# Router row products moved from the routing stage into the two output projections of a flow-matching backbone; filter products in pairs, one root for all filter norms

## The chip, the cores and the metric

One core of one Trainium2 chip runs the whole program. The metric is device time in microseconds (us). The kernel before takes 2402.25 us, the median of 3 runs (2401.37 to 2402.26). Five engines work side by side: TensorE (PE; its weight loads are shown as PEld), VectorE (DVE), ScalarE (ACT), GpSimd (POOL) and SyncE (SP), which here issues most of the DMA transfers. They meet by semaphores.

## The reference, cut to what matters

A trunk of two layers, an mLSTM layer and a Hyena layer, on 512 latent tokens of 1024 features (768 tokens with the context in the first). Behind each layer comes a feed-forward network of 32 experts; a router picks two experts for each token.

```python
def rmsnorm(x, g):
    y = x * rsqrt(mean(x * x, axis=-1) + EPS)
    return y * g

def hyena_filters(L, w1, b1, freq, w2, b2, w3, decay):   # two filters of 1024 channels, 512 taps
    z = sin(freq * (feat @ w1 + b1))                      # 64 wide
    z = sin(freq * (z @ w2 + b2))
    z = z @ w3                                            # 64 -> 2048
    filt = z * exp(-tau[:, None] * decay[None, :])
    return filt * rsqrt(sum(filt * filt, axis=0) + EPS)   # one norm for each channel

def moe_ffn(xt, rg_w, rg_b, re_w, re_b, w13, w2):         # xt: rmsnorm, scale, shift of the rows
    g_prob = softmax(xt @ rg_w + rg_b)                    # 4 groups
    e_logits = (xt @ re_w + re_b)                         # 32 experts, those of the best group count
    e_w, e_idx = top_k(softmax(e_logits_of_group), 2)
    ...                                                   # each token through its two experts:
    y = (silu(x @ w13[e][:, :512]) * (x @ w13[e][:, 512:])) @ w2[e]
```

## The kernel before

Everything is f32, and each product of 128x512 is two MATMUL instructions in the trace. The residual stream `hl` stays in SBUF as [128, 4, 1024]: token tile t (128 tokens) and features. The program is a sequence of stages; each ends with a barrier of all engines, and its order is written out by hand for each engine.

**Layer-0 projection (stage c4, from L1860).** PE multiplies the mixer's output `yT` with `m_out_w` into banks 0 to 3, a bank for each token tile, for feature half n = 0 and then n = 1 (`project`, L1974; `ow` is the weight in four pieces, the first of which lies in `uT`). DVE multiplies each bank with the gate and adds it to `hl` (`add_projection`, L1932 and L1934). In the first half PE also makes the Hyena filters: 16 tiles of 128 taps x 512 channels, each a product over 64 rows (`filter_tile`, L1985); DVE multiplies with the envelope `E`, ACT squares the tile (L1910), and PE sums the squares over the taps with a matrix of ones (`square_column`, L1992). Then DVE takes for each of four channel groups an inverse root of a 128x512 tile (`rsqrt`, L100 to L105) and scales four filter tiles (L1956 to L1960), and SP stores them. SP's small loads stand at the start (L1876 to L1886), and PE's first product waits for them.

**Routing (`route`, L235 on).** SP issues nine loads of 2 MB at the start, the weights of the first three experts (six halves of w13, three of w2), and two small ones, and has nothing else to do. PE turns `hl` tile by tile (L320), DVE copies the turned tiles, PE multiplies them with the scaled router weights (`logits`, L314) and the shift (L326). ACT squares the rows for the norm (L293), DVE takes the root, ACT scales the rows (L296) and stores them for the gathers (L299). From the logits DVE works out the two experts of each token and a table of slots (L373 to L472, from L378 on unchanged by the edit), and POOL gathers the first three blocks of rows (L218).

**Experts (`experts`, L474 on).** There are 36 steps for 32 experts (four experts have two steps) and some more for overflow. Each step turns the gathered rows (L592), multiplies with w13 (L602), turns the hidden block (L610) and multiplies with w2 (L622). SP loads the weights on (`load_w13`, L521; `load_w2`, L526), each load when PE has done with the buffer that it takes. A seventh buffer `w13x` exists only in this stage, and its load waits for nothing.

```python
q, hq = (2 * p + h - NH) // 2, (2 * p + h - NH) % 2
sp.wait_ge(S["up" if hq else "upa"], LAST[q] + 1)
```

**Hyena (`hyena_mix`, L754 on).** Its end is the output projection `project` (L1078) into eight banks, bank g = 2t + n. `residual` (L182, its operations at L189 and L190) adds them to `hl` as they come. After it stands the routing stage of layer 1, and after its experts the final norm.

## Time and profile before

| what | value |
|---|---|
| median of 3 runs | 2402.25 us |
| profiled execution: its own time | 2399.6 us |
| its span | 2397.7 us |
| PE busy | 2071.9 us, 86% |
| DVE busy | 847.0 us, 35% |
| ACT busy | 357.2 us, 15% |
| POOL busy | 237.9 us, 10% |
| DMA, mean over the span | 247 GB/s |

Times in all rows are from the start of the span. PE is the busiest engine over the whole, but the mean hides stages with different limits: the page's slices show 419 GB/s of DMA through most of both expert stages and next to none in the projections. In slices, layer 0's projection lies at 721 to 877 us, its routing at 878 to 938, its experts to about 1434, Hyena to 1820, routing 1 from 1822 to 1881 and its experts to about 2360. A busy share near 1 of PE with a granted clock of 0.50 is half speed: there the same work takes twice as long.

### The profile page before, as it was taken

Reading aid. Unit: us, or ns where it says so; the run is one execution under the profiler, and the core shown is the slowest. Engines: PE = TensorE matmul, PEld = TensorE weight load, DVE = VectorE, ACT = ScalarE, POOL = GpSimd, SP = SyncE. Lnnn points to the kernel's source line nnn. Section 1 sums busy time; section 2 is a strip of 40 time slices with the busy share of each in tenths; the row PEclk is TensorE's granted clock in tenths of the full one; section 3 lists DMA queues with packets and bytes.
Section 4 is the critical chain, followed back from the end, with each engine's and each line's share of the span. In section 5 each row is a group of like instructions: output and inputs, shape, how many; then the busy total and the mean of one; then the engine's idle time right before and its main releaser. Section 6 shows DMA issues by size and latency. Waiting matters only on the chain. (4 is left out here: it accounts for less than half of the span.)

```text
span 2397.7 us, 20742 instructions
## 1 busy us (share of the span) xinstructions
PE 2071.9 (86%) x7536; PEld 923.4 (39%) x7536; DVE 847.0 (35%) x1645; ACT 357.2 (15%) x754; POOL 237.9 (10%) x525
## 2 busy tenths in 40 slices
PE   5999999999949984999797967999997699888882
PEld 2555344444423352443232323444455244323330
DVE  2776401356351574222111214264744322211113
ACT  2111203122201110111111101211101111111111
POOL 0000000000000001222121210000000122112120
PEclk9999999999979976999999998999997799999996
DMA  9897504211003048999999975112015899999994
GB/s 340 297 377 280 199 36 149 97 62 62 1 2 132 18 182 345 397 419 420 419 419 419 414 275 206 53 53 70 18 71 237 338 405 419 419 420 419 419 416 171
DMA packets 182887, 592.82 MB, mean 247 GB/s; under 512 B 23464, under 2 KB 40608, under 8 KB 175401
## 3 DMA queue, kind: packets, MB, share of 16 engines
...
q14 instruction: 51, 0.42, 0.1%
HBM read 571.87 MB, written 42.31 MB: 256 GB/s over the span
## 5 line engine op out<-in xcount | busy, mean ns | idle before, releaser
L602 PE MATMUL bank<-w,xT0e 128*64 128x512 f32 x976 | 222.9, 603 | 24.0 <-DMA w<-in_moe_w 21.0
L602 PE MATMUL bank<-w,xT1e 128*64 128x512 f32 x944 | 215.0, 603 | 21.6 <-DMA w<-in_moe_w 18.7
L1063 PE MATMUL bank<-uhi,wnh 128*128 128x512 f32 x384 | 168.4, 593 | 0.9 <-ACT uhi L842 0.9
L622 PE MATMUL bank<-w,hT0e 128*64 128x512 f32 x592 | 139.8, 614 | 26.6 <-DMA w<-in_moe_w 22.4
L622 PE MATMUL bank<-w,hT1e 128*64 128x512 f32 x576 | 134.9, 610 | 26.6 <-DMA w<-in_moe_w 22.4
L602 PEld LDWEIGHTS bank<-w,xT0e 128*64 128x64 f32 x976 | 78.7, 139 | 162.2 <-issue 136.8
L602 PEld LDWEIGHTS bank<-w,xT1e 128*64 128x64 f32 x944 | 76.4, 139 | 154.2 <-issue 131.4
L1412 PE MATMUL bank<-uT,wo 128*128 128x512 f32 x256 | 132.0, 597 | 0.8 <-ACT uT L1224 0.8
L1749 PE MATMUL bank<-uT,wo 128*128 128x512 f32 x256 | 110.7, 593 | 0.0
L698 DVE COPY hT0e<-bank 128x256 f32<-128x256 f32 x37 | 15.7, 424 | 258.6 <-PE bank L610 258.6
L698 DVE COPY hT1e<-bank 128x256 f32<-128x256 f32 x36 | 15.3, 424 | 258.9 <-PE bank L610 258.9
L1063 PEld LDWEIGHTS bank<-uhi,wnh 128*128 128x128 f32 x384 | 71.8, 190 | 86.9 <-issue 85.8
L1323 DVE SCALAR_TENSOR_TENSOR acc<-adab,cv,acc 128x2048 f32<-128x2048 f32 x35 | 82.2, 2350 | 16.9 <-DMA adab<-in_ada_w 16.1
L218 POOL DMA_INDIRECT xg<-d_v,gix x79 | 83.8, 1061 | 40.6 <-issue 40.6
L1974 PE MATMUL bank<-ow,yT 128*128 128x512 f32 x192 | 84.5, 593 | 0.0
L1800 PE MATMUL bank<-vw,xmh 128*128 128x512 f32 x192 | 83.0, 592 | 0.0
L622 PEld LDWEIGHTS bank<-w,hT0e 128*64 128x64 f32 x592 | 45.0, 140 | 97.7 <-issue 71.7
L622 PEld LDWEIGHTS bank<-w,hT1e 128*64 128x64 f32 x576 | 43.4, 140 | 95.0 <-issue 69.3
L1413 PE MATMUL bank<-uT,wo 128*128 128x256 f32 x256 | 76.1, 379 | 0.0
L676 ACT ACTIVATE sg0e<-bank 128x256 f32<-128x256 f32 x37 | 14.2, 384 | 405.1 <-PE bank L602 405.1
L1561 POOL TENSOR_SCALAR_AFFINE_SELECT PW<-PW 128x128 f32<-128x128 f32 x32 | 10.8, 343 | 630.3 <-ACT PW L1619 629.0
L1413 PEld LDWEIGHTS bank<-uT,wo 128*128 128x128 f32 x256 | 48.6, 190 | 61.2 <-issue 61.2
...
## 6 DMA issues: line engine op xcount, KB each, us to landing
...
```

Of the source, the lines that this page charges most:

```text
L218: g.indirect_dma_start(xg[u][:], None, d_v[l].rearrange("s (h d) -> (s h) d", h=2), bass.IndirectOffsetOnAxis(gix[u][:, 0:1], 0), bounds_c ...
L602: ins = t_.matmul(b[n * C:(n + 1) * C, :].rearrange("c (g f) -> c g f", g=2), xT[:, k, half * C:(half + 1) * C], w13s[i][:, k, n], start=( ...
L622: ins = t_.matmul(b_y[m * C:(m + 1) * C, :], hT[:, k, half * C:(half + 1) * C], w2[:, u, kk, m * 512:(m + 1) * 512], start=(kk == 0), stop ...
L676: a.activation(sg[:], b_gu[u][:, 0:DE // 2], ACT.Silu).then_inc(S["sg"], 1)
L698: v.tensor_copy(hT[:].rearrange("p k n -> p (k n)"), b_h[:, 0:2 * P]).then_inc(S["hT"], 1)
L1063: ins = t_.matmul(bank[i % 2][:], wn[:, q % 2, k, f * P:(f + 1) * P], uh[:, k, :], start=(k == 0), stop=(k == KD - 1))
L1323: ins = v.scalar_tensor_tensor(out=a_, in0=w, scalar=s, in1=a_, op0=ALU.mult, op1=ALU.add)
L1412: t_.matmul(bank[2 * (i % 2)][:], w, uT[:, k, CTX:NTOK], start=(k == 0), stop=(k == KD - 1))
L1413: ins = t_.matmul(bank[2 * (i % 2) + 1][:, 0:CTX], w, uT[:, k, 0:CTX], start=(k == 0), stop=(k == KD - 1))
L1749: ins = t_.matmul(bank[n % 4][:], wo[h % 2][:, k, f * P:(f + 1) * P], uT[:, k, CTX:NTOK], start=(k == 0), stop=(k == KD - 1))
L1800: ins = t_.matmul(b, xmh[:, f, c0:c0 + P], vw[:, f, :], start=(f == 0), stop=(f == FT - 1))
L1974: ins = t_.matmul(bank[t][:], yT[:, i * FT + f, t * P:(t + 1) * P], ow[i][:, f, n * 512:(n + 1) * 512], start=(i == 0 and f == 0), stop=(i ...
```

## The change

The routing stage loses the squares, the row turns, the copies, the router products and the root. They move into the two projections, row tile by row tile: as soon as tile t of `hl` is complete, ACT squares it, PE turns it (`turn_rows`: eight transposes into two banks), ACT and DVE copy one bank each, and PE multiplies with the router weights (`row_logits`: eight products of 36 columns, 16 instructions). The router weights are scaled in place (`router_rows`), `shift_logits` multiplies the shift, and `row_scales` takes the root of the four row norms. For this the second half of layer 0's projection goes through the token tiles one after the other, where it went through the four weight pieces in the outer loop. In the Hyena stage the turns stand between and behind the last banks. The filter products of two channel groups go side by side: their 64 rows lie in the lower and in the upper half of the array, into two banks, so `fw2`, its biases and `fw3` are loaded into both halves, with five more small loads. The squares are added up on DVE in `acc4`, four products with 32 columns of ones sum all four groups into one bank, one `rsqrt` of 128x512 serves all, and four products of one row each spread its result over the partitions. The logits stay in one bank (6 or 0) across the stage's end.

In the diff indentation is shortened.

```diff
+NR = NGRP + NE
+LGB = (6, 0)
+A2c = sbt(top, "A2c", [P, KD]);
+rss = sbt(top, "rss", [P, TL]); rst = [sbt(top, f"rst{i}", [P, TL]) for i in range(2)]
+s_rwa = [sem(f"s_rwa{l}") for l in range(2)]
...
-def residual(dve, own, src, ready, gate, tmp):
+def router_rows(dve, own, l, rwS):
...
+  own(v.scalar_tensor_tensor(out=A2c[:], in0=scale, scalar=1.0, in1=gain, op0=ALU.add, op1=ALU.mult))
+  own(v.tensor_tensor(rwS, rw[:], shift.rearrange("p (k o) -> p k o", o=1).to_broadcast(wide), ALU.mult))
+  v.tensor_tensor(rw[:], rw[:], A2c[:].rearrange("p (k o) -> p k o", o=1).to_broadcast(wide), ALU.mult).then_inc(s_rwa[l], 1)
...
+def row_scales(dve, own):
+  v = nc.vector
+  own(v.tensor_scalar(rss[:], rss[:], 1.0 / D, EPS, ALU.mult, ALU.add))
+  rsqrt(v, own, rst[0][:], rss[:], rst[1][:])
...
+def turn_rows(t, lo, hi):
+  for k in range(KD):
+    ins = nc.tensor.transpose((hi if k >= KH else lo)[:, k % KH * P:(k % KH + 1) * P], hl[:, t, k * P:(k + 1) * P], ident[:])
...
+def row_logits(t, rows, dst):
+  for k in range(KD):
+    ins = nc.tensor.matmul(dst[:, t * NR:(t + 1) * NR], rows[:, k, :], rtab[0][0][:, k, :], start=(k == 0), stop=(k == KD - 1))
...
+def shift_logits(dst, rwS):
+  for k in range(KD):
+    ins = nc.tensor.matmul(dst[:, TL * NR:(TL + 1) * NR], ones[:], rwS[:, k, :], start=(k == 0), stop=(k == KD - 1))
...
-        at_least(act, S["sq"], t)
-        a.activation(junk, hl[:, t, :], ACT.Square, accum_out=ss[:, t:t + 1]).then_inc(S["sq"], 1)
-      act.wait_ge(S["rstd"], 1)
-      for t in range(TL):
-        a.activation(vt[:, t, :], hl[:, t, :], ACT.Copy, scale=ss[:, t:t + 1]).then_inc(S["vsc"], 1)
+        a.activation(vt[:, t, :], hl[:, t, :], ACT.Copy, scale=rss[:, t:t + 1]).then_inc(S["vsc"], 1)
...
-      def logits(k):
-        pe.wait_ge(S["hTv"], k + 1)
-        if k == 0:
-          pe.wait_ge(S["rwa"], 1)
-        for t in range(TL):
-          ins = t_.matmul(bank[2 + t][:, 0:NR], hT[:, k % 2, t * P:(t + 1) * P], rwA[:, k, :], start=(k == 0), stop=(k == KD - 1))
-        return ins.then_inc(S["lps"], 1)
...
-        v.tensor_copy(hT[:, k % 2, :], bank[k % 2][:]).then_inc(S["hTv"], 1)
-        if k == 5:
-          dve.wait_ge(S["sq"], TL)
-          own(v.tensor_scalar(ss[:], ss[:], 1.0 / D, EPS, ALU.mult, ALU.add))
-          rsqrt(v, own, r1[:], ss[:], r2[:])
-          own(v.tensor_copy(r1[:], ss[:]))
-          v.memset(r2[:], 0.0).then_inc(S["rstd"], 1)
...
+      own(v.tensor_tensor(cst[:], lgb[:, TL * NR:(TL + 1) * NR], rb[:], ALU.add))
+      for t in range(TL):
+        lg = lgb[:, t * NR:(t + 1) * NR]
+        v.scalar_tensor_tensor(out=LG[:, t, :], in0=lg[:, 0:NGRP], scalar=rss[:, t:t + 1], in1=cst[:, 0:NGRP], op0=ALU.mult, op1=ALU.add)
+        own(v.scalar_tensor_tensor(out=LE[:, t, :], in0=lg[:, NGRP:NR], scalar=rss[:, t:t + 1], in1=cst[:, NGRP:NR], op0=ALU.mult, op1=ALU.add))
...
+      for t in range(TL):
+        act.wait_ge(S["ro"], t + 1)
+        at_least(act, S["ln"], t)
+        a.activation(rjunk, hl[:, t, :], ACT.Square, accum_out=rss[:, t:t + 1]).then_inc(S["ln"], 1)
+        act.wait_ge(S["tn"], t + 1)
+        at_least(act, S["lg"], t - 1)
+        a.activation(turned[t % 2][:, 0:KH, :].rearrange("p k n -> p (k n)"), bank[2 * t][:], ACT.Copy).then_inc(S["tcA"], 1)
...
-      residual(dve, own, bank, S["o"], g1, A)
+      router_rows(dve, own, 1, rwS)
+      def turned_rows(t):
+        dve.wait_ge(S["tn"], t + 1)
+        at_least(dve, S["lg"], t - 1)
+        v.tensor_copy(turned[t % 2][:, KH:KD, :].rearrange("p k n -> p (k n)"), bank[2 * t + 1][:]).then_inc(S["tcV"], 1)
+      for t in range(TL):
+        for n in range(2):
+          cs = slice(n * 512, (n + 1) * 512)
+          dve.wait_ge(S["o"], 2 * t + n + 1)
+          own(v.tensor_tensor(A[:, n, :], bank[2 * t + n][:], g1[:, cs], ALU.mult))
+          ins = v.tensor_tensor(hl[:, t, cs], hl[:, t, cs], A[:, n, :], ALU.add)
+          if n == 0:
+            own(ins)
+          else:
+            ins.then_inc(S["ro"], 1)
+        if t >= 2:
+          turned_rows(t - 2)
+      turned_rows(TL - 2)
+      turned_rows(TL - 1)
+      dve.wait_ge(S["ln"], TL)
+      row_scales(dve, own)
...
+      def turn(t):
+        pe.wait_ge(S["ro"], t + 1)
+        turn_rows(t, bank[2 * t], bank[2 * t + 1]).then_inc(S["tn"], 1)
+      def logits(t):
+        pe.wait_ge(S["tcA"], t + 1)
+        pe.wait_ge(S["tcV"], t + 1)
+        row_logits(t, turned[t % 2], bank[LGB[1]]).then_inc(S["lg"], 1)
       for g in range(4, 8):
         project(g, range(KD)).then_inc(S["o"], 1)
+        if g == 5:
+          turn(0)
+        if g == 6:
+          pe.wait_ge(s_rwa[1], 1)
+          logits(0)
+          turn(1)
+      logits(1)
+      turn(2)
+      shift_logits(bank[LGB[1]], rwS)
+      logits(2)
+      turn(3)
+      logits(3)
...
-    sp.dma_start(fw2[:], I["h_f_w2"][0]).then_inc(s_fld, 16)
-    for i, k in enumerate(("h_f_b1", "h_f_b2", "h_f_freq")):
-      sp.dma_start(pc[:, i:i + 1], I[k].rearrange("o p -> p o"), allow_slow_non_contiguous=True).then_inc(s_fld, 16)
-    sp.dma_start(fw3[:], I["h_f_w3"][0]).then_inc(s_dec, 16)
+    for h in range(2):
+      sp.dma_start(fw2[:, h, :], I["h_f_w2"][0]).then_inc(s_fld, 16)
+      for i, k in enumerate(("h_f_b1", "h_f_b2", "h_f_freq")):
+        sp.dma_start(pc[h * HFH:(h + 1) * HFH, i:i + 1], I[k].rearrange("o p -> p o"), allow_slow_non_contiguous=True).then_inc(s_fld, 16)
+    for h in range(2):
+      sp.dma_start(fw3[h * HFH:(h + 1) * HFH, :], I["h_f_w3"][0][:, h * D:(h + 1) * D]).then_inc(s_dec, 16)
...
+    for j in range(NP4):
+      n, t = pair(j)
+      if j + 1 < NP4:
+        envelopes(j + 1)
+      act.wait_ge(s_g, 2 * j + 2)
+      at_least(act, s_ac4, n * (TL - 1) + max(t - 1, 0))
+      for h in range(2):
+        a.activation(sqt[:, h, :] if t else acc4[:, n + 2 * h, :], tile(n + 2 * h, t), ACT.Square).then_inc(s_sq4, 1)
+    for t in range(TL):
+      act.wait_ge(s_hl4, t + 1)
+      at_least(act, s_ln, t)
+      a.activation(junk, hl[:, t, :], ACT.Square, accum_out=rss[:, t:t + 1]).then_inc(s_ln, 1)
+      act.wait_ge(s_tn, t + 1)
+      at_least(act, s_lg, t - 1)
+      a.activation(turned[t % 2][:, 0:KH, :].rearrange("p k n -> p (k n)"), bank[4][:], ACT.Copy).then_inc(s_tcA, 1)
...
-    def square_sum(n):
-      dve.wait_ge(s_sm, TL * n + TL)
-      v.tensor_scalar(fsum[:, n, :], bank[6 + n % 2][:], EPS, None, ALU.add).then_inc(s_smv, 1)
...
+    def square_sums(j):
+      n, t = pair(j)
+      dve.wait_ge(s_sq4, 2 * j + 2)
+      if t > 0:
+        for h in range(2):
+          ins = v.tensor_tensor(acc4[:, n + 2 * h, :], acc4[:, n + 2 * h, :], sqt[:, h, :], ALU.add)
+        ins.then_inc(s_ac4, 1)
...
-    for n in range(4):
-      dve.wait_ge(s_smv, n + 1)
-      r = fsum[:, n, :]
-      rsqrt(v, own, kx[:], r, ft[:])
...
+    dve.wait_ge(s_sm, 1)
+    own(v.tensor_scalar(rn, bank[4][:], EPS, None, ALU.add))
+    dve.wait_ge(s_x4, 32)
+    add_projection(0, 0)
+    add_projection(0, 1)
+    rsqrt(v, own, kx, rn, rtmp)
+    v.memset(pc[:, 0:1], 0.0).then_inc(s_rn, 1)
+    add_projection(0, 2)
+    add_projection(0, 3)
+    add_projection(1, 0)
+    normalised(0)
+    normalised(1)
+    normalised(2)
+    add_projection(1, 1)
+    turned_rows(0)
+    normalised(3)
+    for t in range(2, TL):
+      add_projection(1, t)
+      turned_rows(t - 1)
+    turned_rows(TL - 1)
+    dve.wait_ge(s_ln, TL)
+    row_scales(dve, own)
...
-    def filter_tile(i):
-      n, t = i // TL, i % TL
-      if i == 0:
+    def filter_pair(j):
+      n, t = pair(j)
+      if j == 0:
         pe.wait_ge(s_zz, 2)
-        pe.wait_ge(s_dec, 64)
-      at_least(pe, s_g, i - 1)
-      t_.matmul(bank[4 + i % 2][:], z[1][:, t * P:(t + 1) * P], fw3[:, n * 512:(n + 1) * 512], start=True, stop=True).then_inc(s_zps, 1)
-    def square_column(i):
-      n, t = i // TL, i % TL
-      pe.wait_ge(s_sq4, i + 1)
-      if t == 0:
-        at_least(pe, s_smv, n - 1)
-      t_.matmul(bank[6 + n % 2][:], ones[:], sqf[:], start=(t == 0), stop=(t == TL - 1)).then_inc(s_sm, 1)
+        pe.wait_ge(s_dec, 80)
+      at_least(pe, s_g, 2 * j - 2)
+      for h in range(2):
+        rows = slice(h * HFH, (h + 1) * HFH)
+        t_.matmul(bank[4 + 2 * (j % 2) + h][:], z1[rows, t * P:(t + 1) * P], fw3[rows, n * 512:(n + 1) * 512], start=True, stop=True).then_inc(s_zps, 1)
     groups = [(i, t) for i in range(HEADS) for t in range(TL)]
-    pe.wait_ge(s_fld, 16 * 6)
+    pe.wait_ge(s_fld, 160)
     t_.matmul(bank[4][0:HFH, :], fw1[:], ft[0:HEMB, :], start=True, stop=True).then_inc(s_zps, 1)
     for g, (i, t) in enumerate(groups):
       project(0, i, t)
-      if g == 2:
+      if g == 1:
         pe.wait_ge(s_zz, 1)
-        t_.matmul(bank[4][0:HFH, :], fw2[:], z[0][:], start=True, stop=True).then_inc(s_zps, 1)
-      if g >= FIRST:
-        filter_tile(g - FIRST)
-      if g >= FIRST + 1:
-        square_column(g - FIRST - 1)
-    done = len(groups) - FIRST
-    for i in range(done, NT4):
-      filter_tile(i)
-      square_column(i - 1)
-    square_column(NT4 - 1)
-    for i, t in groups:
-      project(1, i, t)
+        t_.matmul(bank[4][:], fw2[:].rearrange("p h n -> p (h n)"), z0[0:HFH, :], start=True, stop=True).then_inc(s_zps, 1)
+      if FIRST <= g < FIRST + NP4:
+        filter_pair(g - FIRST)
+      if g == FIRST + NP4 + 1:
+        pe.wait_ge(s_ac4, 2 * (TL - 1))
+        for n in range(4):
+          ins = t_.matmul(bank[4][32 * n:32 * n + 32, :], ones[:, 0:32], acc4[:, n, :], start=True, stop=True)
+        ins.then_inc(s_sm, 1)
+    for t in range(TL):
+      for i in range(HEADS):
+        project(1, i, t)
+      if t == 0:
+        pe.wait_ge(s_rn, 1)
+        for n in range(4):
+          t_.matmul(bank[4 + n][:], ones[32 * n:32 * n + 1, :], rn[32 * n:32 * n + 1, :], start=True, stop=True).then_inc(s_bc, 1)
+      else:
+        pe.wait_ge(s_hl4, t)
+        pe.wait_ge(s_fin, 2)
+        at_least(pe, s_tcA, t - 1)
+        at_least(pe, s_tcV, t - 1)
+        turn_rows(t - 1, bank[4], bank[5]).then_inc(s_tn, 1)
+      if t >= 2:
+        pe.wait_ge(s_tcA, t - 1)
+        pe.wait_ge(s_tcV, t - 1)
+        if t == 2:
+          pe.wait_ge(s_fin, 3)
+        row_logits(t - 2, turned[t % 2], bank[LGB[0]]).then_inc(s_lg, 1)
+    pe.wait_ge(s_tcA, TL - 1)
+    pe.wait_ge(s_tcV, TL - 1)
+    row_logits(TL - 2, turned[TL % 2], bank[LGB[0]]).then_inc(s_lg, 1)
+    pe.wait_ge(s_hl4, TL)
+    turn_rows(TL - 1, bank[4], bank[5]).then_inc(s_tn, 1)
+    shift_logits(bank[LGB[0]], rwS)
+    pe.wait_ge(s_tcA, TL)
+    pe.wait_ge(s_tcV, TL)
+    row_logits(TL - 1, turned[(TL - 1) % 2], bank[LGB[0]]).then_inc(s_lg, 1)
```

On PE, in the first half of layer 0's projection, the filter products (`fw3`) and square sums (`onesmat`) stood between the projection groups like this (x4 counts four products):

```order
L1974 MATMUL bank1<-ow1,yT 128x512 x4
L1985 MATMUL bank4<-fw3,z1 128x512
L1974 MATMUL bank2<-ow1,yT 128x512 x4
L1985 MATMUL bank5<-fw3,z1 128x512
L1992 MATMUL bank6<-sqf,onesmat 128x512
L1974 MATMUL bank3<-ow1,yT 128x512 x4
L1985 MATMUL bank4<-fw3,z1 128x512
L1992 MATMUL bank6<-sqf,onesmat 128x512
```

and now, at the same place (`front` holds `z1`):

```order
L2068 MATMUL bank0<-ow1,yT 128x512 x4
L2081 MATMUL bank4<-fw3,front 128x512
L2081 MATMUL bank5<-fw3,front 128x512
L2068 MATMUL bank1<-ow1,yT 128x512 x4
L2081 MATMUL bank6<-fw3,front 128x512
L2081 MATMUL bank7<-fw3,front 128x512
L2068 MATMUL bank2<-ow1,yT 128x512 x4
```

The 16 square sums are gone, and the filter products stand two and two. The same stage ended on PE with projection groups and the barrier; it now ends like this (`hl` turned with `ident`, `rw` the router weights, `rwS` the shift):

```order
L2068 MATMUL bank3<-ow3,yT 128x512 x4
L208 MATMUL bank4<-ident,hl 128x128 x4
L208 MATMUL bank5<-ident,hl 128x128 x4
L214 MATMUL bank6<-rw,front 128x36 x16
L208 MATMUL bank4<-ident,hl 128x128 x4
L208 MATMUL bank5<-ident,hl 128x128 x4
L220 MATMUL bank6<-rwS,onesmat 128x36 x8
L214 MATMUL bank6<-rw,front 128x36 x8
```

Two turns, three sets of row products and the shift stand behind the last projection. In the Hyena stage PE's end was two banks of projection and the barrier:

```order
L1078 MATMUL bank6<-uhi,x2i 128x512 x4
L1078 MATMUL bank6<-wnh,x2i 128x512 x4
L1078 MATMUL bank7<-uhi,x2i 128x512 x4
L1078 MATMUL bank7<-wnh,x2i 128x512 x4
L758 UNCONDITIONAL_BRANCH
```

and is now:

```order
L1095 MATMUL bank7<-uhi,x2i 128x512 x4
L1095 MATMUL bank7<-wnh,x2i 128x512 x4
L214 MATMUL bank0<-rw,Pri 128x36 x8
L208 MATMUL bank4<-ident,hl 128x128 x4
L208 MATMUL bank5<-ident,hl 128x128 x4
L220 MATMUL bank0<-Bi,onesmat 128x36 x8
L214 MATMUL bank0<-rw,Pri 128x36 x8
L208 MATMUL bank6<-ident,hl 128x128 x4
L208 MATMUL bank7<-ident,hl 128x128 x4
L214 MATMUL bank0<-rw,Pri 128x36 x8
```

Behind the last projection bank stand two turns, three sets of row products and the shift.

## Rows read from the trace of the kernel before

**Rows 1.** Windows: stretch, its us, busy by engine, PEclk, DMA share, GB/s.

```profile
930.00:1000.00 70.00, 58.37 (x266) 23.32 (x268) 12.35 (x37) 10.95 (x30) 15.17 (x33) 0.89 0.88 338
...
1870.00:1960.00 90.00, 77.24 (x357) 31.57 (x356) 17.08 (x55) 13.00 (x36) 21.31 (x45) 0.90 0.92 355
1960.00:2300.00 340.00, 302.39 (x1405) 115.61 (x1404) 63.84 (x183) 43.53 (x130) 73.67 (x156) 0.98 1.03 419
```

**Rows 2.** Timeline of PE, last products of experts 0: start, duration, idle before.

```profile
1424.25 3.65 PE L622 MATMUL bank<-w,hT0e 128*64 128x512 f32 x16 [0.89 <-DMA w<-in_moe_w]
```

**Rows 3.** Timeline of SP: issues in both routing stages and behind them.

```profile
878.16 0.92 SPq L263 DMA_DIRECT2D w<-in_moe_w  x2
...
913.89 5.61 SPq L266 DMA_DIRECT2D g2h<-d_mod  x2
938.96 0.40 SPq L521 DMA_DIRECT2D w13x0e<-in_moe_w  x1
...
1858.12 5.57 SPq L266 DMA_DIRECT2D g2h<-d_mod  x2
1881.98 0.40 SPq L521 DMA_DIRECT2D w13x1e<-in_moe_w  x1
```

**Rows 4.** Timeline of DVE and POOL, routing of layer 0.

```profile
903.72 0.17 DVE L378 TENSOR_REDUCE gs0r<-LG0r 128x4 f32<-128x16 f32 x1
...
933.69 1.04 POOL L218 DMA_INDIRECT xg<-d_v,gix  x1 [0.50 <-issue]
```

**Rows 5.** Timeline of SP and PE, start of layer 0's projection.

```profile
717.72 1.23 SPq L1880 DMA_DIRECT2D pc<-in_h_f_b  x2
...
721.32 1.97 PE L1996 MATMUL bank<-ft,fw 33*64 33x512 f32 x2 [9.40 <-DMA pc<-in_h_f_freq]
```

**Rows 6.** Timeline of PE and DVE, layer 0's projection.

```profile
802.73 1.12 PE L1992 MATMUL bank<-sqf,onesmat 128*128 128x512 f32 x2
803.78 1.12 PE L1985 MATMUL bank<-fw,z 64*128 64x512 f32 x2
...
815.18 1.13 PE L1992 MATMUL bank<-sqf,onesmat 128*128 128x512 f32 x2 [0.78 <-ACT sqf L1910]
...
829.87 41.36 PE L1974 MATMUL bank<-ow,yT 128*128 128x512 f32 x96
...
876.50 0.69 DVE L1934 TENSOR_TENSOR hl<-hl,tmp 128x512 f32<-128x512 f32 x1
```

**Rows 7.** Groups by line and shape: count, busy us, mean ns, idle before.

```profile
L1016 PE MATMUL bank<-idfti,Pri 128*128 128x256 f32 x64 | 14.3, 382 | 1.0 <-ACT zb1i L861 1.0
...
L1016 PE MATMUL bank<-idfti,Pri 64*128 64x256 f32 x64 | 7.2, 379 | 0.0
```

**Rows 8.** Timeline of PE: short products at the half clock, turns at the full.

```profile
882.70 1.76 PE L314 MATMUL bank<-rwA0r,hT0r 128*128 128x36 f32 x8
...
959.43 0.60 PE L592 MATMUL bank<-ident,xg 128*128 128x128 f32 x4
```

**Rows 9.** Windows of 2 us: PE's granted clock after Hyena's projection.

```profile
1820.00:1822.00 2.00, 0.01 (x1) 0.04 (x1) 0.01 (x1) 0.04 (x1) 0.06 (x1) 1.00 0.02 4
...
1824.00:1826.00 2.00, 2.00 (x11) 2.00 (x12) 0.27 (x1) 1.94 (x5) 0.47 (x4) 0.50 0.92 373
```

**Rows 10.** Timeline of PE and DVE, end of the Hyena stage.

```profile
1814.84 3.60 PE L1078 MATMUL bank<-wnh,x2i 128*128 128x512 f32 x8
...
1819.27 0.69 DVE L190 TENSOR_TENSOR hl<-hl,Ai 128x512 f32<-128x512 f32 x1
```

**Rows 11.** Timeline of DVE: root of row norms, root of a 128x512 tile, a copy.

```profile
890.91 0.16 DVE L362 TENSOR_SCALAR ss0r<-ss0r 128x4 f32<-128x4 f32 x1
...
893.67 0.16 DVE L105 SCALAR_TENSOR_TENSOR ss0r<-r20r,r10r 128x4 f32<-128x4 f32 x1
...
820.39 0.42 DVE L100 TENSOR_SCALAR kx<-fsum 128x512 int32<-128x512 int32 x1
...
829.29 0.69 DVE L105 SCALAR_TENSOR_TENSOR fsum<-ft,kx 128x512 f32<-128x512 f32 x1
```

More of the change, by code:

```diff
@@ L200, in expert_ffn @@
                 g2h = sbt(c, f"g2h{l}", [P, D // 2])
-                A2c = sbt(c, f"A2c{l}", [P, KD])
                 xg = [sbt(c, f"xg{l}{u}", [P, D // 2]) for u in range(NB)]
@@ L370, in _ @@
                     own(v.tensor_scalar(hp2[:], hp[:], 2.0 * NO_ROW, None, ALU.add))
-                    dve.wait_ge(S["lps"], KD)
-                    for t in range(TL):
-                        v.scalar_tensor_tensor(out=LG[:, t, :], in0=bank[2 + t][:, 0:NGRP], scalar=r1[:, t:t + 1], in1=cst[:, 0:NGRP], op0=ALU.mult, op1=ALU.add)
-                        own(v.scalar_tensor_tensor(out=LE[:, t, :], in0=bank[2 + t][:, NGRP:NR], scalar=r1[:, t:t + 1], in1=cst[:, NGRP:NR], op0=ALU.mult, op1=ALU.add))
                     def first_max(x, n, mx, scratch, hot):
@@ L1864, in build, with tile, pair @@
             MAGIC = 1.5 * 2.0 ** 23
-            NT4 = 4 * TL
-            FIRST = 5
+            NP4 = 2 * TL
+            FIRST = 4
             blk = c4.enter_context(nc.Block())
-            def tile(i):
-                n, t = i // TL, i % TL
+            def tile(n, t):
                 return fl[n // 2][:, t, (n % 2) * 512:(n % 2 + 1) * 512]
+            def pair(j):
+                return j // TL, j % TL
             @blk.sync
@@ L1917, in _ @@
                 own = Counter(dve, s_d4)
[L1918 to L1919 removed]
+                router_rows(dve, own, 0, rwS[:])
+                dve.wait_ge(s_fld, 160)
+                for i, (z, rows) in enumerate(((z0, HFH), (z1, P))):
+                    zr, kr = z[0:rows, :], kx[0:rows, :]
                     dve.wait_ge(s_zps, i + 1)
[L1921 to L1926 removed]
@@ L1940, in _ @@
-                for i in range(NT4):
-                    dve.wait_ge(s_zps, 3 + i)
-                    dve.wait_ge(s_E, i + 1)
-                    v.tensor_tensor(tile(i), bank[4 + i % 2][:], E[:, i % 2, :], ALU.mult).then_inc(s_g, 1)
-                    if i % TL == 1 and i > TL:
-                        square_sum(i // TL - 1)
-                dve.wait_ge(s_x4, 32)
-                add_projection(0)
-                square_sum(3)
-                for n in range(4):
-                    dve.wait_ge(s_smv, n + 1)
-                    r = fsum[:, n, :]
-                    rsqrt(v, own, kx[:], r, ft[:])
+                    own(v.tensor_scalar(zr, bank[4][0:rows, :], pc[0:rows, i:i + 1], pc[0:rows, 2:3], ALU.add, ALU.mult))
```

159 lines of the change are left out of this document (76 added, 83 removed).

## The prediction, written before the changed kernel ran

> **What bounds the kernel now.** I read the page's slices first, since the mean busy shares mix stages, and then asked for windows by stage. In the expert stages DMA runs at 419 GB/s [rows 1], and at their end PE waits for each load that it uses: its last products begin 0.89 us after a weight landed [rows 2]. So an expert stage ends when its bytes have come, and what counts is when their stream starts and whether it pauses. It does pause once a layer. SP has issued its nine big loads and two small ones by 913.89 + 5.61 = 919.50, and issues the next one at 938.96, when the routing stage is over [rows 3]. From 930 to 1000 the rate is 338 GB/s for 419: 70 x (1 - 338/419) = 13.5 us lost. In layer 1, from 1870 to 1960, it is 90 x (1 - 355/419) = 13.7 us [rows 1]. By the busy share of the DMA engines (0.88 and 0.92 for 1.03) the loss is 10.2 and 9.6 us. The projections move almost no weights: there PE sets the time, with the last DVE additions behind it [rows 6, 10], and every microsecond put behind the last projection delays the start of the next stream.
>
> **Layer 0's routing.** The chain on DVE reaches its first choice of a group at 903.72, 25.5 us after the stage began [rows 3, 4]. The edit leaves of that a constant, eight short operations and three around them, some 3 us. So the third gather, which ended at 933.69 + 1.04 = 934.73 [rows 4], would end 22.5 us earlier, at 912.2. The stage doesn't win 22.5 us: SP is busy issuing until 919.50, since its loads wait for room in the queue, and the barrier needs SP too. The next load was issued 4.2 us after POOL's end (938.96 - 934.73) and so comes at about 919.5 + 4.2 = 923.7, which is 15.3 us earlier. The nine loads were still landing at 930 (pause of 13.5 us or less, closed by then), so the queue isn't empty. The load after that needs half a step of PE, some 8 us, to 932, while `w13x` (2 MB, 5.0 us at 419 GB/s) carries the stream to about 937. I expect no pause, and take 12.5 us of gain for each layer, between 9.6 and 13.7. It can't be less than nothing, nor more than the pause: the 15 us by which PE starts earlier go into PE's waits for weights.
>
> **Layer 0's projection, start.** PE's first product waits for the last small load. There are four more before it (a second `fw2` and three columns) at 0.6 us each, two of them taking 1.23 [rows 5]: +2.4 us. The router rows on DVE stand ahead of that and are covered by it.
>
> **Layer 0's projection, PE.** Filter product and square sum stand 1.05 us apart (802.73 to 803.78) where two instructions of a dense projection take 41.36 / 96 x 2 = 0.86: about 0.2 us a change of shape [rows 6]. 32 of them cost 33.6 us, and with the wait of 0.78 [rows 6] 34.4 go. What comes:
> - eight filter pairs. In Hyena's inverse transform 64 products over 64 rows in alternating halves take 7.2 us and 64 over all 128 rows 14.3 [rows 7]: two halves run at once. So a pair costs one product, 8 x 1.05 = 8.4 us; 16.8 if they don't overlap, the other end.
> - sums with 32 columns, and the spreading over one row: four at once would be 1.1 us each; nothing overlapping, 4.2 each. I take 1.3 and 1.5, near the first, as the strips are again disjoint.
> - two turns. Four transposes take 0.60, of which a last one is 0.27: 0.11 us each, eight 1.1 [rows 8]; two turns 2.2 us.
> - one set of row products: at half clock eight instructions take 1.76, about 0.2 each [rows 8]; at full clock half of that, 16 x 0.1 + 0.2 = 1.8 us.
> - six more changes of shape: 1.2 us.
>
> Together 16.4 us. PE's last projection, which ended at 829.87 + 41.36 = 871.2 [rows 6], ends at 871.2 + 2.4 - 34.4 + 16.4 = 855.6.
> The one root left costs DVE 9.6 us (820.39 to 829.29 + 0.69, [rows 11]) and has as cover the last two projection groups of half 0 and token tile 0 of half 1, 48 instructions at 0.43 or 20.7 us; the three roots that go free DVE of 29 us. The store of the filters now ends before the last token tile. Where DVE were late after all, PE would wait at `s_rn`, by 9.6 us at most.
>
> **Layer 0's projection, tail.** Before, the stage ended at 876.50 + 0.69 = 877.2 [rows 6], 6.0 us behind PE. Now stand behind PE's last projection a turn (1.1), two sets of row products (3.6), a turn, the shift and the last set. Here the clock matters. Behind Hyena's projection it was granted 1.00 until 1822 and 0.50 from 1824 on, although PE was busy 2.00 of 2.00 us with turns and short products [rows 9]: the higher level, 2.4 GHz, was lost 5 us behind the last dense product and these didn't bring it back. So I take full clock for 5 us, and 1.9 + 3.5 + 3.5 at the half for the rest: 13.6 us, and the stage ends at 869.2, earlier by 8.0. At full clock all through the last item is DVE's row scales at 3 us [rows 11]: 10.1 us.
>
> **Hyena's tail.** Between banks 5 and 7 stand a turn, a set and a turn: 1.1 + 1.8 + 1.1 = 4.0 us. Behind bank 7 the copy of tile 1 is queued on DVE behind bank 7's additions, so PE waits 2.2 us for it (two additions of 0.7 and a copy of 0.7); then, mostly at the half clock, set 2.6, turn 1.9, shift 3.5, set 3.5, turn 1.9, copy 0.8, set 3.5: 19.9 us. Before, DVE ended at 1819.27 + 0.69, 1.5 us behind PE's 1818.4 [rows 10]. The start of the last stream moves by 4.0 + 19.9 - 1.5 = 22.4; at full clock by 4.0 + 13.6 - 1.5 = 16.1. I take 21, near the first.
>
> The Trainium skill, TensorE: Matmul & The Clock Gate, Part 1, says that the throttled state is the default and that it comes back when the engine has idled; a stream of short products isn't idleness. By that rule alone both tails keep the full clock.
> The rows have both an idle stretch of 3.5 us and short products ahead of the fall, so they don't decide it. It is a rival below.
>
> **The sum.** -8.0 - 12.5 + 21 - 12.5 = -12.0 us. The profiled execution took 2399.6 us (span 2397.7 and 1.9 around it), the median is 2.65 above it; taken from the median: 2402.25 - 12.0 = 2390.2 us. The gain stands on the two pauses and on layer 0's projection; layer 1 alone gives 8.5 us back.
>
> **Rivals.**
> - The tails keep the full clock. Hyena's tail 16.1 for 21, layer 0's 3.5 less: -20.4, 2382 us. For it: no idle stretch of 3.5 us is left; against it: PE waits 2.2 us behind bank 7, and short products ran 20 us without raising the clock.
> - The clock also falls in midstream, or PE waits there: turns and a set, 2.9 us of short products, now stand twice between dense groups in layer 0 and once in Hyena. Each fall costs up to a dense tile's first 3 to 4 us again: 3 x 3 = 9 us, -3, 2399 us.
> - The halves don't overlap: 8.4 + 2.9 + 2.7 = 14 us more, +2, 2404 us. [rows 7] speak against it.
> - Slower: the stream's pause stays. The loads behind `w13x` need a buffer that PE has left; were PE's first step late (a gather behind nine queued loads, say), the pause would only move. With nothing won there: -8.0 + 21 = +13, 2415 us. It decides for slower from the point where both pauses together shrink by less than 13 us. Against it: in the full stream PE waits for weights, not for gathered rows [rows 2], and 923.7 lies ahead of the pause.
>
> **How the numbers follow.** The forecast has 0.50 with its own range from -20 to -5. Full clock in the tails has 0.20, falls in midstream 0.13, no overlap 0.07, the pause that stays 0.10. The measurement tells 0.2% from nothing, which is 4.8 us. Faster by more: 0.46 + 0.20 + 0.04 = 0.70. Within: 0.04 + 0.08 + 0.05 = 0.17. Slower: 0.01 + 0.02 + 0.10 = 0.13. The range runs from 2378 (full clock, and pairs and sums at their best) to 2408, where the pause half stays, with the last case mostly left out.
>
> **What would show it.** SP's first load of the expert stage within 6 us of its last small one in both layers (before, 18.2 us in layer 1 too: 1881.98 after 1858.12 + 5.57 [rows 3]), and no pause in the stream behind it; the filter pairs at about 1.05 us for four instructions; PE's last projection of layer 0 at about 856 and the stage's end near 869; Hyena's end some 20 us further from its last bank, with the clock at 0.50 in it; PE's waits for weights in the experts longer by some 15 us a layer. The forecast is wrong if the stream still pauses, if DVE is late with the root, or if the tails are longer than 14 and 20 us.

## The result and the profile after

| | before | after |
|---|---|---|
| median | 2401.81 us (2399.72 to 2402.48, 8 runs) | 2408.77 us (2406.59 to 2410.41, 8 runs) |
| span of the profiled execution | 2397.7 us | 2406.8 us |
| ratio after / before | | 1.0031, 95% interval 1.002 to 1.0042 |

The changed kernel is slower by 7.0 us, where 12.0 us of gain were forecast; the time lies 0.8 us above the range of 2378 to 2408 us. (The kernel before has the three runs of 2402.25 us and five later ones in this median.) By stage, each from SP's first issue in it to the first one in the next (us, from both traces):

| stage | before | after | difference | forecast |
|---|---|---|---|---|
| all ahead of layer 0's projection | 716.4 | 718.5 | +2.1 | 0 |
| layer 0's projection | 161.8 | 149.3 | -12.5 | -8.0 |
| routing and experts, layer 0 | 565.5 | 564.6 | -0.9 | -12.5 |
| Hyena | 378.3 | 399.1 | +20.8 | +21 |
| routing and experts, layer 1 | 547.6 | 546.9 | -0.7 | -12.5 |
| the rest | 28.2 | 28.3 | +0.1 | 0 |

The sum is +8.9, of a span 9.1 us longer. The first row moves without the edit: in the kernels of the experiments below this stage begins at 716.1 to 719.6 us. Two terms failed, both of them the gain in the expert stages. Yet the pauses did close. SP's timeline in the routing of layer 0 and of layer 1, which answers to [rows 3]:

```profile
867.87 0.92 SPq L291 DMA_DIRECT2D w<-in_moe_w  x2
...
905.80 5.62 SPq L294 DMA_DIRECT2D g2h<-d_mod  x2
913.59 0.41 SPq L506 DMA_DIRECT2D w13x0e<-in_moe_w  x1
...
1868.51 6.10 SPq L294 DMA_DIRECT2D g2h<-d_mod  x2
1876.55 0.40 SPq L506 DMA_DIRECT2D w13x1e<-in_moe_w  x1
```

The next load comes 913.59 - 911.42 = 2.2 us after the last small one, where it was 19.5 us. The windows of the changed kernel, to be held against [rows 1]:

```profile
930.00:1000.00 70.00, 68.85 (x320) 27.80 (x318) 14.05 (x41) 10.07 (x30) 14.22 (x30) 0.97 1.03 409
1870.00:1960.00 90.00, 77.85 (x358) 31.40 (x360) 16.57 (x50) 14.32 (x40) 17.05 (x36) 0.93 1.03 403
1960.00:2300.00 340.00, 293.63 (x1356) 110.80 (x1354) 61.36 (x175) 41.94 (x125) 71.08 (x150) 0.97 1.03 409
```

The last two columns hold the lesson. The DMA share is 1.03 from the start, so there is no pause. But 1.03 now moves 409 GB/s and no longer 419, also deep in the stage, where the edit changed nothing. The page's slices show the same: 409 where 419 stood. Of the 4096-byte packets of the weight loads between 1100 and 1300 us, 99.6% were recorded with 159 ns before, with a mean of 159.4; after, 40% are, and the mean is 163.2. PE stands behind them, as its longest waits show (us in total, times, longest), the kernel before first:

```profile
PE bank L622 <- DMA w<-in_moe_w: 44.7, 29, 4.9
PE bank L602 <- DMA w<-in_moe_w: 39.7, 31, 2.1
```

```profile
PE bank L607 <- DMA w<-in_moe_w: 56.7, 32, 5.3
PE bank L587 <- DMA w<-in_moe_w: 47.6, 34, 2.2
```

The same bytes at 409 for 419 take 2.4% longer, some 12 us of a stream of 500 us, as much as the closed pause is worth.

One thing the edit does to the weight buffers: `A2c`, `rss` and two `rst` are four new small tiles in the outermost pool, 32 bytes each per partition, and every later tile starts 128 bytes higher. The first weight buffer starts at byte 37120 of a partition before, which is 145 x 256, and at 37248 after, 128 past a multiple of 256.

### The profile page after: what moved, and what is told of

Its sections match the earlier page's. It is cut to its first block and busy times, and to the rows that moved or that the text cites. A ratio compares the mean times of both kernels' runs of the same rounds, so it can differ in the third digit from the quotient of the medians.

```text
span 2406.8 us, 20662 instructions
## 1 busy us (share of the span) xinstructions
PE 2043.7 (85%) x7520; PEld 902.5 (37%) x7520; DVE 818.7 (34%) x1601; ACT 361.5 (15%) x762; POOL 238.8 (10%) x525
## 5 line engine op out<-in xcount | busy, mean ns | idle before, releaser
L607 PE MATMUL bank<-w,hT1e 128*64 128x512 f32 x576 | 138.5, 624 | 32.8 <-DMA w<-in_moe_w 28.3
L577 PE MATMUL bank<-ident,xg 128*128 128x128 f32 x300 | 46.2, 277 | 33.7 <-PEq L122 33.7
L661 ACT ACTIVATE sg1e<-bank 128x256 f32<-128x256 f32 x36 | 13.9, 385 | 400.7 <-PE bank L587 400.7
## 6 DMA issues: line engine op xcount, KB each, us to landing
wo<-in_m_in_w SPq DMA_DIRECT2D x4, 2048.0 KB, 10.7
```

The source lines that it names most:

```text
L577: ins = t_.transpose(b_x[k // 2][:, (k % 2) * P:(k % 2 + 1) * P], xg[u][:, k * P:(k + 1) * P], ident[:])
L607: ins = t_.matmul(b_y[m * C:(m + 1) * C, :], hT[:, k, half * C:(half + 1) * C], w2[:, u, kk, m * 512:(m + 1) * 512], start=(kk == 0), stop ...
```

## Experiments on the place of the buffers

Theory A: the stream is slower because its destinations don't start on a multiple of 256 bytes. Rivals: the edit's own work in the experts' time (its routing leaves them another start), or the place of the inputs in HBM, which no SBUF address changes.
Of this the Trainium skill, DMA: Bandwidth & Descriptors, "How a descriptor splits into AXI transactions", says that a descriptor goes in transactions of at most 256 bytes, each read from a multiple of 256, so that one with another start fetches some bytes for nothing; it counts the cost in beats of 32 bytes. It says this of what is read, not of the place in SBUF that a load writes. Carried over to that place, estimates by that page are 132 beats for 128 and 159.4 x 132 / 128 = 164.4 ns at a start 128 bytes off, and 129 beats and 160.6 ns at 32 bytes off; 17 transactions for 16, each at the same price, would be 169 ns. The runs below have 164.1 ns at 128 bytes and 164.0 at 32. So they agree with the period of 256 and the sign, with the beats at 128 bytes but not at 32, and with 169 ns at neither; the measured times count.

**e1, e2: the kernel before, moved by 128 and by 256 bytes.**

```diff
         rtab = []
+        filler = sbt(top, "filler", [P, 32])   # e1; [P, 64] in e2
         wts = sbt(top, "wts", [P, 2, TL])
```

e1, expected:


> The kernel before with one unused tile of 128 bytes per partition ahead of the router tables, so that every later tile, the weight buffers among them, lies 128 bytes further on, as in the changed kernel. Theory A (the lost 13 us a layer are a slower weight stream, 409 for 419 GB/s, and what slows it is where the buffers lie in SBUF): the stream of this kernel falls to about 409 GB/s too, and it takes 24 to 29 us more than before, about 2427 us. Rival B (the stream is slowed by something the edit does in the stages: the earlier stores of the scaled rows, the fuller queue, the earlier start of PE): 419 GB/s and no change, 2402 us within 3.

e2, expected:


> The kernel before with an unused tile of 256 bytes per partition at the same place. Theory A in the form that only the position within 256 bytes counts: 419 GB/s and the time of before, 2402 us within 3. Theory A in the form that the exact place matters in another way (a larger period, or the end of a bank): slower than before by 5 us or more. Rival B: no change either.

Measured: e1 2424.29 us, ratio 1.0093 (1.008 to 1.0107); e2 2400.25 us, ratio 0.9998 (0.9989 to 1.0007), beside a kernel before at 2400.46 us. The filler does no work at all and costs 24 us; twice the filler costs nothing. The windows of e1 and then of e2:

```profile
1960.00:2300.00 340.00, 294.83 (x1371) 111.26 (x1369) 62.97 (x181) 43.51 (x130) 71.11 (x150) 0.98 1.03 408
```

```profile
1960.00:2300.00 340.00, 302.34 (x1406) 115.58 (x1404) 63.86 (x182) 43.64 (x130) 73.95 (x156) 0.98 1.03 419
```

**e3, e4: the changed kernel, put back on the old places.** e3 adds the same 128 bytes (with the edit's own 128 they make 256). e4 adds no tile (shortened):

```diff
-        A2c = sbt(top, "A2c", [P, KD])
-        rss = sbt(top, "rss", [P, TL]); rst = [sbt(top, f"rst{i}", [P, TL]) for i in range(2)]
+        A2c = colH[:, P - KD:P]; rss = lambda: rtab[0][1][:, NR:NR + TL]   # rb is wider by TL
+        rst = [wts[:, i, :] for i in range(2)]
```

e3, expected:


> The changed kernel with an unused tile of 128 bytes per partition ahead of the router tables, so that the weight buffers lie 256 bytes from their place before. Theory A with a period of 256 bytes: 419 GB/s, and the changed kernel's gain appears: 2409 - 26 = 2383 us. Rival B: 409 GB/s stays and the time is that of the changed kernel, 2409 us within 3.

e4, expected:


> The changed kernel with its small new tiles put into unused columns of others, so that uT, the mixer's weights and the nine weight buffers have exactly the addresses of before. Theory A: 419 GB/s in both expert stages, 2380 to 2386 us. Rival B: 409 GB/s and 2409 us within 3. A third theory, that the 409 GB/s come from where the runtime puts the inputs in HBM for another program, expects e1 unchanged or by chance either way, and this one as likely slow as fast.

Measured: e3 2385.5 us, ratio 0.9933 (0.992 to 0.9947); e4 2382.77 us, ratio 0.9927 (0.9913 to 0.994). So the forecast's gain is there once the buffers stand where they stood: -17.7 us in e4, more than the 12.0 forecast, since in e4 both tails ran for the most part at the full clock (below); that comes near the first rival, which had -20.4. Its windows, for [rows 1] again:

```profile
930.00:1000.00 70.00, 68.85 (x330) 28.39 (x328) 14.75 (x42) 10.04 (x30) 15.09 (x33) 1.00 1.03 419
1870.00:1960.00 90.00, 84.93 (x398) 34.68 (x396) 18.62 (x54) 13.39 (x40) 19.22 (x42) 0.98 1.03 412
1960.00:2300.00 340.00, 298.38 (x1390) 113.50 (x1388) 63.15 (x181) 43.52 (x130) 72.86 (x154) 0.98 1.03 419
```

Routing and experts are 565.5 - 552.6 = 12.9 us shorter than before in layer 0 and 547.6 - 535.6 = 12.0 in layer 1 (forecast 12.5 each). This decides for theory A against the edit's own work, which e3 and e4 keep. The place of the inputs in HBM was not varied by itself, but it would have to follow the SBUF addresses by chance: in the window 1960 to 2300 all seven kernels whose w13 and w2 buffers start on a multiple of 256 move 418 or 419 GB/s, and the four in which none of them does (the changed kernel, e1, e5, e9) 407 to 409.

**e5, e6, e9, e10: which bytes, and which tiles.** All four are the kernel before with filler. e5 has 32 bytes (`[P, 8]`) in e1's place; the others have 128 bytes inside the expert stage:

```diff
+                fillera = sbt(c, f"fillera{l}", [P, 32])   # e9, e10
                 w13 = sbt(c, f"w13_{l}", [P, NH - 1, KH, 2 * DE])
+                fillerb = sbt(c, f"fillerb{l}", [P, 32])   # e6, e10
                 w2 = sbt(c, f"w2_{l}", [P, NB, DE // P, D])
```

e5, expected:


> The kernel before with 32 unused bytes ahead of the small tiles, so that each later tile moves by 32 bytes; work and order are before's. If every start of a 4096-byte packet off a multiple of 256 bytes costs the same (the packet then covers 17 pieces of 256 bytes in place of 16), this is as slow as 128 bytes: 407 to 409 GB/s in the experts, about 164 ns a packet, 2424 us, 24 above before. If only the half of a 256-byte block counts (two places that alternate, told by bit 7 of the address), nothing changes: 2400 us. If the price grows with the distance, about 2406.

e6, expected:


> The kernel before with 128 unused bytes between w13 and w2 of an expert stage: the w2 buffers and the small tiles behind them start at 128 mod 256, the w13 buffers stay at 0, and no tile of any other stage moves. A third of the expert bytes goes to w2. If the place of each load's own destination sets its packets' time, w2's loads take about 164 ns a packet and w13's 159, and the time is 24 / 3 = 8 us over before, 2408 us. If what counts is another tile than the weight buffers (hl, the projections' or Hyena's buffers), nothing changes, 2400 us; if one slow load in three slows them all, 2424 us.

e9, expected:


> The kernel before with 128 unused bytes ahead of w13 of both expert stages: only tiles of these stages move, the w13 and w2 buffers to 128 mod 256; hl, the projections' and Hyena's tiles stay. If the places of the weight buffers are the whole cause: as e1, 2424 us, 24 above before. If the tiles of the other stages or the table tiles had a part in e1: less, down to 2400 us if they had all of it.

e10, expected:


> The kernel before with 128 unused bytes ahead of w13 and 128 more between w13 and w2 of an expert stage: w13 starts at 128 mod 256, w2 at 0. Two thirds of the expert bytes go to w13, in two loads of 2 MB behind each other, then comes one of w2. If each load pays for its own place: 2/3 of 24, 2416 us (but then e6 with w2 alone should have cost 8 and cost 2). If the price falls only on a load off a multiple of 256 behind another such one, half of w13's loads pay: about 12 us, 2412 us. If what e6 did not cost is all in w13: 22 us, 2422 us.

| kernel | off a multiple of 256 | time, us | against before | packets at 159 ns, mean ns |
|---|---|---|---|---|
| e2 | none of w13, w2 | 2400.25 | 0.9998 (0.9989 to 1.0007) | 99.6%, 159.5 |
| e5 | all, by 32 | 2426.44 | 1.0106 (1.009 to 1.0121) | 13%, 164.0 |
| e9 | all, by 128 | 2422.85 | 1.0092 (1.0076 to 1.0108) | 26%, 164.1 |
| e10 | w13 (2 of 3 loads) | 2408.05 | 1.003 (1.0019 to 1.0042) | 72%, 160.9 |
| e6 | w2 (1 of 3 loads) | 2403.08 | 1.0009 (1.0 to 1.0018) | 92%, 160.0 |

Their last windows, e9 first and e10 behind it:

```profile
1960.00:2300.00 340.00, 294.78 (x1364) 111.19 (x1364) 63.06 (x181) 43.60 (x130) 71.03 (x150) 0.97 1.03 408
```

```profile
1960.00:2300.00 340.00, 299.65 (x1393) 114.16 (x1390) 63.11 (x181) 43.51 (x130) 72.65 (x154) 0.98 1.03 415
```

The packets are those from 1100 to 1300 us. e9 moves only tiles of the expert stages and costs 21.9 us, nearly all of e1's: it is the weight buffers (the small tiles behind them move by the same 128 bytes in e6, at 2.1 us). e5 costs as much as e1, so it is not one half of a block that counts; 32 and 128 bytes are the only distances off the multiple that were tried for all buffers. e10 and e6 met none of their expected values: w13 alone costs 7.1 us and w2 alone 2.1 (by its interval hardly clear of nothing; its packets show it better, 92% for 99.6%), together 9, while both together cost 22. Each load paying for its own place (16 and 8) is out. What fits is that a load pays only where the load ahead of it is off as well. In e10 that is the second w13 of each pair, one load in three: 22 / 3 = 7.3. (The expectation's 12 for this case was worked out wrongly: half of w13's loads are a third of all, 8 us.) In e6 it is only where w2 meets `w13x`, which stands at 32 mod 256 there, about one load in ten: 2.2. In the packets of e10 the slow stretches do come back every three loads, in those of e6 about every ten. And `w13x`, itself off the multiple in the kernel before (201632, 160 mod 256), costs nothing that shows between two good ones: its nine loads a layer are nearly a tenth of all, and 99.6% of the packets have 159 ns; in the changed kernel it is the other way round, `w13x` alone is well placed (201728 = 788 x 256), and the packets at 159 ns come about it. This rule of pairs is read from the sizes and the traces after the fact; no run tests it by itself, and why it is so stays open.

## Experiments on the tails

Theory: Hyena's end costs what layer 1's closed pause gives, and its parts are PE's wait for tile 1's copy and the half clock behind it. Rival: the end is DVE's row scales, or it is hidden behind loads.

**e7: e4 with layer 1's router left in its routing stage**, with the code of the kernel before for `l == 1` in `route` and in Hyena's end.

Expected:


> The changed kernel with its weight buffers at before's addresses (e4), and layer 1's router left in its routing stage as in the kernel before; layer 0's projection and routing as changed. By the stages of e4 Hyena gives back 17.4 to 20.8 us and layer 1's routing and experts win 12: without both 2382.8 + 12.0 - 17.4 = 2377.4 us, at most 2374. So about 5 us faster than e4, and 23 to 26 faster than before. If Hyena's longer end were hidden behind the experts' loads (which wait for nothing of it) it would be 12 us slower than e4, 2395 us.

**e8: e4 with Hyena's tail in another order.**

```diff
                             logits(0)
                             turn(1)
-                    logits(1)
+                            shift_logits(bank[LGB[1]], rwS)
                     turn(2)
-                    shift_logits(bank[LGB[1]], rwS)
-                    logits(2)
+                    logits(1)
                     turn(3)
+                    logits(2)
                     logits(3)
```

DVE copies tile 1's rows between the additions of banks 6 and 7. Expected:


> The changed kernel with before's addresses (e4), and in Hyena's tail another order: the eight shift products stand ahead of bank 7's projection, DVE copies tile 1's turned rows ahead of bank 7's additions, and behind bank 7 PE does turn 2, set 1, turn 3, set 2, set 3. In e4 18.8 us pass from the end of bank 7's products to the last set. The theory (the wait of 2.3 us and the clock at half behind it are the price of Hyena's tail): turn 1.0, set 1.9, turn 1.0 (after a wait of at most 0.4), and two sets of 1.9, which is 8.1 us at full clock, and the shift's 1.9 midstream: 18.8 - 8.1 - 1.9 = 8.8 us faster than e4, 2374 us. If the clock falls to half all the same after 5 us behind the last dense product (as forecast), the two last sets take 3.6 each: 5.4 us faster, 2377 us. If the tail is set by DVE's row scales: no more than 1 us faster, 2382 us.

**e11: e8 with layer 0's projection reordered too.** The lines added on PE; the same work goes from behind its last projection, and DVE copies tile 2's turned rows ahead of token tile 3's addition:

```diff
                         project(1, i, t)
+                        if t == 3 and i == 1:
+                            logits(1)
+                            turn(2)
+                            shift_logits(bank[LGB[0]], rwS)
```

Expected:


> e8 (before's addresses, Hyena's tail reordered) with layer 0's projection in another order as well: set 1, turn 2 and the shift stand between the dense groups of token tile 3, and behind PE's last projection only set 2, turn 3 and set 3 are left. In e8 13.0 us passed from the last projection to the stage's end, with the clock at half from 862; in e4 10.2 at mostly full clock. New: 1.9 + 1.0 + at most 1.0 of wait for the copy + 1.9 = 5.8 us, DVE's row scales end at about 6, and the work moved (1.9 + 1.0 + 1.9) is midstream: 13.0 - 6.5 - 4.8 = 1.7 us at full clock all through, plus the 3.5 us that half clock costs e8 there. So 2373 to 2377 us, 2 to 5 us faster than e8. If turn 2 and set 1 wait midstream for the copies: no faster than e8, 2378 us.

Measured: e7 2379.23 us, ratio 0.9911 (0.9895 to 0.9926); e8 2378.45 us, 0.9903 (0.9888 to 0.9919); e11 2376.13 us, 0.9899 (0.9883 to 0.9915). In e7 Hyena takes 379.0 us and layer 1's routing and experts 547.5, about as before (378.3 and 547.6), and in e8 389.7 and 536.5. So even in the better order layer 1's move gives +10.7 - 11.0, nothing: e7 and e8 can't be told apart. In e4, against the same e7, it is +16.7 - 11.9, a loss of 4.8 us. e7 is 1.8 us over its expectation and e8 4.5 over the first of its own, and in both layer 0's projection took 3.3 and 3.1 us more than e4's 149.3, since there the clock fell in its tail (below). Hyena is 6.0 us shorter than in e4 where 8.8 were expected. That expectation began from a wrong number: the 18.8 us from bank 7's last product to the last set are those of the changed kernel (1829.79 - 1811.01). In e4 they are 1813.83 - 1799.11 = 14.7, so the same sum gives 14.7 - 8.1 - 1.9 = 4.7. Against the changed kernel, to which 18.8 belongs, Hyena is 9.4 us shorter for the 8.8.
PE at the end of e8's Hyena stage, from bank 7's products on:

```profile
1800.39 3.60 PE L1098 MATMUL bank<-wnh,x2i 128*128 128x512 f32 x8
1803.83 1.04 PE L209 MATMUL bank<-ident,hl 128*128 128x128 f32 x8
1804.70 1.88 PE L215 MATMUL bank<-rw,Pri 128*128 128x36 f32 x16
1806.40 1.07 PE L209 MATMUL bank<-ident,hl 128*128 128x128 f32 x8
1807.31 4.00 PE L215 MATMUL bank<-rw,Pri 128*128 128x36 f32 x32
```

No wait is left, and PE is done 7.3 us behind bank 7's products: the end is neither DVE's row scales nor hidden, and both rivals are out. e11's stage gains less over e8 than the 2 to 5 us expected: layer 0's projection takes 151.6 us for 152.4, since PE waits 0.87 us for the last copy and the last set again runs at the half clock. Its median does lie 2.3 us below e8's and in the expected 2373 to 2377, but only 0.8 us of that is in the stage that was reordered; this is luck more than foresight. e11 is the fastest kernel measured, by its median 24.8 us faster than the kernel before beside it (2400.93), though its interval overlaps those of e7 and e8.

## Why the prediction was wrong, step by step

**The failed step** is "I expect no pause, and take 12.5 us of gain for each layer", and in it "It can't be less than nothing, nor more than the pause". The pause went, as said. The bound was wrong: the price of the stream itself, 419 GB/s, was carried over from [rows 1] as if the edit could not touch it. The four new tiles moved the weight buffers off a multiple of 256 bytes and took 12.0 us (564.6 - 552.6) in layer 0 and 11.3 (546.9 - 535.6) in layer 1 back. None of the rivals had it. The nearest, "the pause stays", has the right sign (+13 us) by a wrong mechanism: it would have shown a DMA share below 1.

**SP's next load**: forecast 45.5 us behind the stage's start in layer 0 (923.7 - 878.16), measured 45.7. Two misses of 2 us cancel in this: SP was done with its loads 911.42 - 867.87 = 43.6 us behind the start, not 41.3, and the next load came 2.2 us after that, not 4.2. The range of 9.6 to 13.7 us holds e4's 12.9 and 12.0.

**PE's waits for weights**: forecast some 15 us longer a layer. With the old places (e4) they are 46.3 us for 43.4 in layer 0 and 41.7 for 41.1 in layer 1. The forecast counted the same time twice. PE's first step begins 16 us earlier in the stage (911.17 - 867.36 = 43.8 us behind its start, for 937.99 - 878.16 = 59.8), but the stage also ends 12.9 earlier, so only the 3 us between them can go into waits.

**Layer 0's projection**: forecast -8.0, measured -12.5. Start: +2.4 forecast; the stage's first product comes 726.08 - 718.54 = 7.5 us behind its first issue, and before it was 721.32 - 716.4 = 4.9, so +2.6. Pairs, sums, spreading, turn and set, which answer to [rows 6 to 8] (PE's timeline, the changed kernel):

```profile
749.15 1.13 PE L2081 MATMUL bank<-fw,front 64*128 64x512 f32 x4
750.21 3.70 PE L2068 MATMUL bank<-ow,yT 128*128 128x512 f32 x8
...
790.11 1.07 PE L2096 MATMUL bank<-acc,onesmat 128*32 128x512 f32 x8
...
811.90 1.14 PE L2105 MATMUL bank<-sqt,onesmat 1*128 1x512 f32 x8
...
841.42 1.04 PE L208 MATMUL bank<-ident,hl 128*128 128x128 f32 x8
842.29 1.87 PE L214 MATMUL bank<-rw,front 128*128 128x36 f32 x16
...
847.51 10.46 PE L2068 MATMUL bank<-ow,yT 128*128 128x512 f32 x24
857.82 1.04 PE L208 MATMUL bank<-ident,hl 128*128 128x128 f32 x8
858.69 3.66 PE L214 MATMUL bank<-rw,front 128*128 128x36 f32 x32
862.18 1.07 PE L208 MATMUL bank<-ident,hl 128*128 128x128 f32 x8
863.09 1.87 PE L220 MATMUL bank<-rwS,onesmat 128*128 128x36 f32 x16
864.79 2.26 PE L214 MATMUL bank<-rw,front 128*128 128x36 f32 x16
```

Four instructions of a pair fill 1.06 us (750.21 - 749.15), and eight of the sums 0.99: the halves and strips do run at once. PE's last projection ends at 847.51 + 10.46 = 858.0, 2.4 above the forecast 855.6, of which 2.2 came from ahead of the stage. The one root did not hold PE up (811.90 follows without a wait). The mis-sized term is the tail: 13.6 us forecast, and measured 864.79 + 2.26 - 858.0 = 9.1 to the end of PE's last set, which ends last. The rival for full clock had 10.1. The granted clock is the column ahead of the last two; the changed kernel, and then e7:

```profile
864.00:866.00 2.00, 2.00 (x20) 2.00 (x20) 1.65 (x11) 0.00 (x0) 0.00 (x0) 1.00 0.00 0
866.00:868.00 2.00, 1.05 (x7) 0.91 (x6) 0.72 (x7) 0.10 (x1) 0.12 (x1) 0.57 0.00 0
```

```profile
836.00:856.00 20.00, 20.00 (x66) 10.31 (x65) 1.98 (x3) 1.73 (x3) 0.00 (x0) 1.00 0.00 1
...
858.00:860.00 2.00, 2.00 (x20) 2.00 (x20) 0.43 (x1) 1.01 (x2) 0.00 (x0) 1.00 0.00 0
860.00:862.00 2.00, 2.00 (x16) 2.00 (x16) 0.00 (x0) 0.00 (x0) 0.00 (x0) 0.73 0.00 0
862.00:864.00 2.00, 2.00 (x12) 2.00 (x11) 1.59 (x7) 0.60 (x1) 0.00 (x0) 0.50 0.00 0
```

With the same code in this stage, the clock stayed at 2.4 GHz until after 866 in the changed kernel and until about 865.6 in e4, over 8 us behind the last dense product, and fell to 1.2 GHz between 860 and 862 in e7 and e8, 5 us behind it, as forecast; the stage then took 152.6 and 152.4 us, where the forecast by the same measure is 161.8 - 8.0 = 153.8. So the forecast and its rival both occur, 3 us apart. Each of these is one profiled execution; which of the two comes isn't a matter of the kernel alone, since e8's four runs, of one program, took 2375.5 us (mean granted clock 0.945) to 2379.8 (0.941). What decides it is not shown.
The rule cited in the prediction (the Trainium skill, TensorE: Matmul & The Clock Gate, Part 1: the throttled state returns when the engine has idled) does not cover e7: there PE was busy in all of 20.00 us and in 2.00 of every 2.00 behind them, and the clock fell under short products.

**Hyena's tail**: forecast +21, measured +20.8, of 3.5 us between the banks (4.0 forecast) and 18.8 behind bank 7 (19.9). The wait of 2.2 us is 2.27, at the full clock; the half clock came 2 us behind it, about 4 us behind bank 7's last product. In e4, with the same code in this stage, it came only some 8.6 us behind it, 14.7 us were enough, and Hyena took +17.4. So the agreement with 21 is in part luck. This answers to [rows 9, 10]:

```profile
1807.41 3.60 PE L1095 MATMUL bank<-wnh,x2i 128*128 128x512 f32 x8
1813.28 1.95 PE L214 MATMUL bank<-rw,Pri 128*128 128x36 f32 x16 [2.27 <-DVE Pri L967]
1815.06 1.83 PE L208 MATMUL bank<-ident,hl 128*128 128x128 f32 x8
1816.68 3.46 PE L220 MATMUL bank<-Bi,onesmat 128*128 128x36 f32 x16
1819.95 3.61 PE L214 MATMUL bank<-rw,Pri 128*128 128x36 f32 x16
1823.37 1.95 PE L208 MATMUL bank<-ident,hl 128*128 128x128 f32 x8
1826.19 3.60 PE L214 MATMUL bank<-rw,Pri 128*128 128x36 f32 x16 [0.88 <-DVE Pri L967]
```

```profile
1814.00:1816.00 2.00, 2.00 (x16) 2.00 (x16) 0.00 (x0) 0.00 (x0) 0.00 (x0) 0.80 0.03 8
1816.00:1818.00 2.00, 2.00 (x12) 2.00 (x11) 0.69 (x1) 1.07 (x2) 0.00 (x0) 0.50 0.00 0
```

and e4, where bank 7's last product ends at 1799.1:

```profile
1804.00:1806.00 2.00, 2.00 (x22) 2.00 (x19) 0.69 (x1) 1.63 (x3) 0.00 (x0) 1.00 0.00 0
1806.00:1808.00 2.00, 2.00 (x19) 2.00 (x19) 0.00 (x0) 0.00 (x0) 0.00 (x0) 0.93 0.00 0
```

**The other rivals** are out: no dense group in midstream ran slower or waited (3.70 us for eight instructions behind each pair, 3.60 elsewhere), and the halves overlap. PE's first step did begin earlier (912.63), and did not move the end, since PE waits for weights.
